# Rotations ahead of the key and value evictions, G cleared in two parts, and the identity copied before the scores

## The reference, cut to what matters

```python
# RWKV-7, per head of 64: the state S is updated token by token
def step(state, inp):
    r_t, w_t, k_t, v_t, kk_t, a_t = inp
    sa = jnp.einsum('bhij,bhj->bhi', state, -kk_t)
    state = (state * w_t[:, :, None, :] + sa[..., None] * (kk_t * a_t)[:, :, None, :]
             + v_t[..., None] * k_t[:, :, None, :])
    return state, jnp.einsum('bhij,bhj->bhi', state, r_t)

# latent attention: 16 heads, 64 plain + 32 rotated features, values of 64
c = hn @ w_down
cq, ckv, kr = jnp.split(c, [384, 640], axis=-1)
q = (rmsnorm(cq, q_norm) @ w_uq).reshape(b, s, 16, 96)
kv = (rmsnorm(ckv, kv_norm) @ w_ukv).reshape(b, s, 16, 128)
q = jnp.concatenate([q_nope, apply_rope(q_rope, positions)], axis=-1)
k_rope = jnp.broadcast_to(apply_rope(kr[:, :, None, :], positions), (b, s, 16, 32))
k = jnp.concatenate([k_nope, k_rope], axis=-1)
o = causal_softmax_attention(q, k, v, 1.0 / math.sqrt(96))
return o.reshape(b, s, 1024) @ w_o
```

## Time and profile before

| | us |
|---|---|
| median of 3 runs (lowest, highest) | 1560.34 (1556.35, 1560.39) |
| the profiled execution | 1560.42 |
| its span | 1558.7 |
| TensorE busy (share of the span) | 1466.2 (94%) |
| VectorE busy | 897.0 (58%) |
| ScalarE busy | 611.8 (39%) |
| GpSimd busy | 161.8 (10%) |
| mean granted clock of TensorE, share of full speed | 0.958 |

### The profile page before, as it was taken

One profiled execution on the slowest core, in us unless ns is written; L12 is line 12 of the kernel. 1 busy time (PEld: TensorE's weight loads), 2 busy tenths in 40 slices (PEclk: granted clock), 3 DMA queues, 4 the chain that ended last, 5 costly groups with the idle time before them and its releaser, 6 DMA issues.

```text
span 1558.7 us, 25630 instructions
## 1 busy us (share of the span) xinstructions
PE 1466.2 (94%) x10804; PEld 1394.0 (89%) x10804; DVE 897.0 (58%) x1167; ACT 611.8 (39%) x722; POOL 161.8 (10%) x149
## 2 busy tenths in 40 slices
PE   4999999899999999999989998999988889999997
PEld 4999999898899999988878878999988778999997
DVE  4655566583356556632563315866676573766665
ACT  3434444434135443411245113444445364344344
POOL 1000000141000000511110000000041051000023
PEclk8999999999999999999989759999998989999998
DMA  8655655332455555524300013555552602555540
GB/s 267 202 188 179 206 169 189 122 126 82 144 176 167 188 188 188 163 85 148 111 1 1 1 61 130 179 180 182 187 162 91 201 4 93 166 181 184 187 135 28
DMA packets 166200, 219.80 MB, mean 141 GB/s; under 512 B 5451, under 2 KB 147020, under 8 KB 165996
## 3 DMA queue, kind: packets, MB, share of 16 engines
q1 hardware_dynamic: 163472, 216.40, 42.3%
q10 hardware_dynamic: 2652, 2.30, 0.5%
HBM read 217.49 MB, written 1.06 MB: 140 GB/s over the span
## 4 chain that ended last, share of the span: by engine, by line
PE 82%; DVE 9%; ACT 4%; issue 3%; POOL 1%; DMA 0%; ACTq 0%; POOLq 0%; SPq 0%; DVEq 0%
PE ps L863 35%; PE ps L903 15%; PE ps L1000 6%; PE ps L839 5%; PE ps L982 2%; PE ps L849 2%; PE ps L1287 2%; PE ps L823 1%; DVE x_second_part L2091 1%; PE ps L1282 1%; PE ps L971 1%; ACT weights_first_parts L1560 1%; PE ps L1425 1%; PE ps L1293 1%; PE ps L855 1%
## 5 line engine op out<-in xcount | busy, mean ns | idle before, releaser
L2192 DVE TENSOR_TENSOR weights_second_parts<-weight_bays,weights_first_parts 128x2048 fp32r<-128x2048 f32 x132 | 301.2, 2289 | 173.2 <-ACT weights_first_parts L1560 172.8
L1560 ACT ACTIVATE weights_first_parts<-weight_bays 128x2048 fp32r<-128x2048 f32 x132 | 252.1, 1918 | 301.9 <-PE ps L863 191.0
L863 PE MATMUL ps<-x_first_part,weights_first_parts 128*128 128x256 f32 x1488 | 210.1, 284 | 1.7 <-DVE weights_second_parts L2192 1.7
L863 PE MATMUL ps<-x_second_part,weights_first_parts 128*128 128x256 f32 x1488 | 208.8, 283 | 0.0
L863 PE MATMUL ps<-x_first_part,weights_second_parts 128*128 128x256 f32 x1488 | 206.5, 282 | 0.0
L863 PEld LDWEIGHTS ps<-x_first_part,weights_first_parts 128*128 128x128 f32 x1488 | 191.8, 192 | 2.7 <-ACT weights_first_parts L1560 1.9
L863 PEld LDWEIGHTS ps<-x_second_part,weights_first_parts 128*128 128x128 f32 x1488 | 191.9, 191 | 0.0
L863 PEld LDWEIGHTS ps<-x_first_part,weights_second_parts 128*128 128x128 f32 x1488 | 189.6, 190 | 0.0
L903 PE MATMUL ps<-hidden_first_part,weights_first_parts 128*128 128x256 f32 x704 | 141.9, 283 | 5.8 <-ACT weights_first_parts L1560 3.7
L903 PE MATMUL ps<-hidden_second_part,weights_first_parts 128*128 128x256 f32 x704 | 141.8, 283 | 0.0
L903 PE MATMUL ps<-hidden_first_part,weights_second_parts 128*128 128x256 f32 x704 | 139.7, 279 | 0.0
(11 more groups left out here) (413 smaller groups left out, 2220.6 us busy)
## 6 DMA issues: line engine op xcount, KB each, us to landing
weight_bays<-in_w_ffn_in SPq DMA_DIRECT2D x44, 1024.0 KB, 5.1
weight_bays<-in_ffn_w_in SPq DMA_DIRECT2D x44, 1024.0 KB, 5.0
weight_bays<-in_w_ffn_out SPq DMA_DIRECT2D x22, 1024.0 KB, 5.1
weight_bays<-in_ffn_w_out SPq DMA_DIRECT2D x22, 1024.0 KB, 5.0
weight_bays<-in_w_in SPq DMA_DIRECT2D x19, 1024.0 KB, 5.3
weight_bays<-in_hyb_w_in SPq DMA_DIRECT2D x13, 1024.0 KB, 5.3
weight_bays<-in_ple_w_gate SPq DMA_DIRECT2D x8, 1024.0 KB, 5.1
weight_bays<-in_w_out SPq DMA_DIRECT2D x4, 1024.0 KB, 5.8
```

Source lines behind the costliest of these rows:

```text
L863: mm = nc.tensor.matmul(dst, w[:, k, j * P:j * P + width], x[:, k], start=(n + k == 0), stop=(n == 2 and k == KD - 1))
L1560: nc.scalar.activation(hi, raw, ACT.Copy).then_inc(*w_hi_ready.inc(f, g, kind, of - g))
L2192: v.tensor_tensor(lo, raw, hi, ALU.subtract).then_inc(*w_lo_d.inc(f, g, kind, of - g))
```

## The change

It does three things.

1. G is cleared in two parts. Elements 2048 to 8191 are cleared once VectorE has written AR (a new event "ar", at which VectorE waits for itself as it did before by a step), elements 0 to 2047, where lw and cc lie, once Bk and Kk are written ("bk"). Before, all of it waited for "bonus".
2. The copy of the identity into Y stands right behind the bonus product, ahead of the wait for G and of the 16 predicated copies. Before, it stood behind them.
3. VectorE's rotations stand in `keep_up` between the query evictions and those of keys and values. Before, they stood behind all evictions.

```diff
--- before.py
+++ after.py
@@ -578,7 +578,7 @@
         def wait_up(eng, bank_no, event):
 
             eng.wait_ge(*(up_a if bank_no % 2 == 0 else up_d).at(*event))
-        def keep_up(eng, parity, split):
+        def keep_up(eng, parity, split, between=None):
 
             done = (up_a, up_d)[parity]
 
@@ -596,6 +596,8 @@
                     copy(dst, bank(b), t).then_inc(*done.inc("q", b // 2, b % 2))
                     if n < 2:
                         split(6 + n)
+            if between:
+                between()
             for (n, t, half), b in UKV.items():
                 if b % 2 == parity:
                     eng.wait_ge(*used_up_to(("ukv", n)))
@@ -1994,8 +1996,11 @@
                     t = slice(tile, tile + tiles)
                     nc.gpsimd.tensor_tensor(xm[0:rows, t], pfT[0:rows, t, 0:SEQ], pfT[0:rows, t, 1:], ALU.subtract).then_inc(*mix_g.inc(key))
 
-                pool.wait_ge(*pre_d.at("bonus"))
-                nc.gpsimd.memset(G[:].rearrange("p a b c d -> p (a b c d)"), 0.0).then_inc(*mix_g.inc("G"))
+                zeroed = G[:].rearrange("p a b c d -> p (a b c d)")
+                pool.wait_ge(*pre_d.at("ar"))
+                nc.gpsimd.memset(zeroed[:, 2048:], 0.0)
+                pool.wait_ge(*pre_d.at("bk"))
+                nc.gpsimd.memset(zeroed[:, 0:2048], 0.0).then_inc(*mix_g.inc("G"))
 
                 def before(t, *event):
 
@@ -2481,7 +2486,8 @@
                 ar = AR.rearrange("p a c n s -> p (a c) n s")
                 two = lambda t: t.rearrange("p a (c s) -> p (a c) s", c=2)
                 v.tensor_tensor(ar[:, :, 0], two(kk), two(dm0), ALU.mult)
-                step(v.tensor_tensor(ar[:, :, 1], two(xm[:, 0:4]), two(dm), ALU.mult))
+                v.tensor_tensor(ar[:, :, 1], two(xm[:, 0:4]), two(dm), ALU.mult).then_inc(*pre_d.inc("ar"))
+                dve.wait_ge(*pre_d.at("ar"))
                 for j in range(RWT):
                     ins = v.scalar_tensor_tensor(xm[:, j], xm[:, j], col("r_k", j), xm[:, 4 + j], ALU.mult, ALU.mult)
                 ins.then_inc(*pre_d.inc("bonus_terms"))
@@ -2490,6 +2496,7 @@
                 dve.wait_ge(*pre_p.at("bonus"))
                 dve.wait_ge(*pre_d.at("bk"))
                 v.tensor_tensor(bonus[:], ps[:, 4:6].rearrange("p b (a s) -> p (b a) s", a=2), xm[:, 8:12], ALU.mult).then_inc(*pre_d.inc("bonus"))
+                step(v.tensor_copy(Y[:].rearrange("p a b c -> p (a b) c"), ident.unsqueeze(1).to_broadcast([P, 16, P])))
                 dve.wait_ge(*mix_g.at("G"))
                 two_masks = masks[:, BEFORE:UPTO + 1].rearrange("p a b -> p (a b)").unsqueeze(1).to_broadcast([P, 2, 2 * P])
                 for n in range(16):
@@ -2506,7 +2513,6 @@
                     mask = masks[:, n].unsqueeze(1).to_broadcast([P, 4, P])
                     if n == 0:
                         dve.wait_ge(*inv_d.at("scores", 15))
-                        step(v.tensor_copy(Y[:].rearrange("p a b c -> p (a b) c"), ident.unsqueeze(1).to_broadcast([P, 16, P])))
                     for g in range(4):
                         if n == 0:
                             data = G[:, g // 2, g % 2 * 4:g % 2 * 4 + 4, 0]
@@ -2625,15 +2631,18 @@
                 v.tensor_scalar(msq[:, 2:4], ps[:, 7, 2:4], 1.0 / 256, EPS, ALU.mult, ALU.add).then_inc(*mean_ready.inc("latent"))
                 dve.wait_ge(*lat_p.at("kr"))
                 v.tensor_copy(krot, ps[:, 6, 0:64].rearrange("p (a b) -> p a b", a=TT)).then_inc(*lat_d.inc("kr"))
-                keep_up(dve, 1, rest_of_mla)
-                dve.wait_ge(*lat_d.at("kr"))
-                dve.wait_ge(*rot_a.at("rot"))
-                step(rotate(krot, [P, TT, 16], cosv[:], sinv[:]))
-                v.tensor_copy(ktok2[:, :, :, 64:96], krot.unsqueeze(2).to_broadcast([P, TT, MH, 32])).then_inc(*lat_d.inc("rotary_key"))
-                dve.wait_ge(*up_a.at("q", 2, 0))
-                dve.wait_ge(*up_d.at("q", 2, 1))
-                cs, sn = (t.unsqueeze(2).to_broadcast([P, TT, MH, 16]) for t in (cosv[:], sinv[:]))
-                rotate(qtok[:, :, :, 64:96], [P, TT, MH, 16], cs, sn).then_inc(*mla_d.inc("rotated"))
+
+                def rotated():
+                    dve.wait_ge(*lat_d.at("kr"))
+                    dve.wait_ge(*rot_a.at("rot"))
+                    step(rotate(krot, [P, TT, 16], cosv[:], sinv[:]))
+                    v.tensor_copy(ktok2[:, :, :, 64:96], krot.unsqueeze(2).to_broadcast([P, TT, MH, 32])).then_inc(*lat_d.inc("rotary_key"))
+                    dve.wait_ge(*up_a.at("q", 2, 0))
+                    dve.wait_ge(*up_d.at("q", 2, 1))
+                    cs, sn = (t.unsqueeze(2).to_broadcast([P, TT, MH, 16]) for t in (cosv[:], sinv[:]))
+                    rotate(qtok[:, :, :, 64:96], [P, TT, MH, 16], cs, sn).then_inc(*mla_d.inc("rotated"))
+
+                keep_up(dve, 1, rest_of_mla, rotated)
                 mask = mats[:, 2].unsqueeze(1).to_broadcast([P, 2, P])
                 for i in range(MH + 2):
                     if i < MH and i % 2:
```

## The result

| | before | after |
|---|---|---|
| median, us (lowest, highest; runs) | 1559.2 (1556.35, 1560.39; 4) | 1544.86 (1542.53, 1546.54; 4) |
| the profiled execution, us | 1560.42 | 1546.54 |
| its span, us | 1558.7 | 1544.8 |
| mean granted clock | 0.958 | 0.966 |

The ratio is 0.991 (95% interval 0.9889 to 0.993): the changed kernel is 0.9% faster, some 14 us. The forecast was 1545.4 us with a range of 1541 to 1551.

A forecast was written before the change was run, and what follows sets the result against it. TensorE held 82% of the chain, so only its waits on VectorE or GpSimd could be won. Terms 9.3 (hybrid mixer) + 5.2 (rotations) + 0.5 (clock) = 15.0 us off 1560.42 gave 1545.4 us, range 1541 to 1551.

The forecast's parts named there:

- clearing and identity copy: first predicated copy sooner: Hybrid mixer, scores: clearing leaves the path, identity copy goes ahead; first predicated copy moves from 782.23 to 776.47, gaining 5.8 us.
- 16 copies at TensorE's full pace: Hybrid mixer, scores: TensorE keeps its full clock, so the predicated copies take 10.0 us instead of 11.3, gaining 1.3 us.
- last copy to the transposes: Hybrid mixer, behind the scores: without the identity copy there, transposes start 1.0 us behind the last copy, not 2.1; gain 1.1 us.
- transposes to M1, by the clock: Hybrid mixer: the clock probably stays up at the 16 transposes, which take about 2.3 us instead of 3.46; 1.1 us taken.
- rotations: first head sooner: Latent attention: rotations run between evictions, so TensorE waits only for the last evictions and starts the first head 5.2 us sooner.
- clock in the first heads: Latent attention, behind the rotations: a full clock after the shorter pause saves between 0 and 2.5 us; 0.5 us taken.
- Port blocked: Rival at the scores: the clearing blocks VectorE's bonus terms at the SBUF port; 2.9 us lost, 1548.3 us; 15%.
- Clock falls in both places as before: Rival at scores and rotations: only the waits go, 8.2 + 5.2 = 13.4 us, giving 1547.0 us; 20%.
- Clock stays down longer: Rival in the inverse's levels: TensorE at the lower clock, matmuls grow by 30 to 50 us, net 1560 to 1580; 3%.
- gain swallowed: Rival at the scores or first head: another, unpriced wait takes most of the gain; about 1553 to 1557 us; 7%.
- both near rivals together: SBUF port blocked at the scores and clock falling at scores and rotations, both at once: 1549.5 us, inside the range.
- The slower rival: Rival in the inverse's levels: the clock stays low there and the kernel ends at 1560 to 1580 us; 3%.

The follow-up runs named there:

- rot_longer: The changed kernel with eight unused 128x512 VectorE products added behind the rotations; median 1543.94 us, ratio 0.9923.
- ident_in_clear: The changed kernel with the identity copy moved right behind the product into Kk, while GpSimd's clearing is under way; median 1542.01 us, ratio 0.9874.
- ident_only: The kernel before with only the identity copy put ahead of the wait for G, still cleared in one piece; median 1556.45 us, ratio 0.9989.
- fill_short: The kernel before with unused matmuls in TensorE's waits, 12 ahead of the fifth pair's scores and 10 ahead of the first head; median 1557.16 us, ratio 0.9987.
- hyb_parts: The kernel before with the clearing in two parts and the identity copy ahead of the scores, rotations as before; median 1547.55 us, ratio 0.994.
- rot_only: The kernel before with only the rotations moved ahead of the key and value evictions; median 1551.53 us, ratio 0.996.

## Why the prediction was right

| term | forecast | measured | by which rows |
|---|---|---|---|
| clearing and identity copy: first predicated copy sooner | 5.8 | 5.85 | 8.24 to 2.39 |
| 16 copies at TensorE's full pace | 1.3 | 1.43 | 11.28 to 9.85 |
| last copy to the transposes | 1.1 | 1.16 | 2.08 to 0.92 |
| transposes to M1, by the clock | 1.1 | 1.02 | 4.25 to 3.23 |
| **sum to the first M1** | **9.3** | **9.46** | 25.85 to 16.39 |
| rotations: first head sooner | 5.2 | 5.24 | 18.24 to 13.00 |
| clock in the first heads | 0.5 | 1.36 | 44.26 to 42.90 |
| **sum of both places** | **15.0** | **16.06** | |

**Point by point.** The clearings took 5.22 and 1.80 us (5.2 and 1.8 forecast) and were over before the bonus product. The slack of the first group of evictions was 2.92 us by VectorE's wait, 2.98 by rot_longer (2.7 forecast). The wait ahead of the first head is 1.80 us. Each term of waiting was right to 0.1 us, because each came from two rows of the same trace whose distance only the order of the work sets.

**The term that was mis-sized** is the clock in the first heads: "Between 0 and 2.5 I take 0.5 us". It measured 1.36. My reasons for the low end were that each head also passes through the other engines, and that the clock might fall in the shorter pause too. Against the first, at the lower level the pace of the first heads was TensorE's (busy 5.00 of 5.00 us), and only at the higher one did TensorE have time to spare (busy 3.24 of 5.00). Against the second, the clock was kept through the pause of 1.8 us.

**The rivals.** *Port blocked* (15%): the bonus terms and both products took their usual times beside a clearing, and ident_in_clear shows on one timeline that the product passes and a copy doesn't. *Clock falls in both places as before* (20%): it did not, in either. At the transposes the table gives the reason more firmly than I had it. In the five kernels that copy the identity behind the scores, TensorE pauses twice (some 1.3 and 1.1 us) and the step to M1 takes 4.1 to 5.2 us; in the eight that copy it ahead, it pauses once and the step takes 3.22 to 3.24. I had argued from the length of the pause alone; the runs show that taking the second of two away decides here: ident_only keeps the long pause ahead of the scores and doesn't lose the clock at the transposes, fill_short has no long pause and loses it. *Clock stays down longer* (3%) and *gain swallowed* (7%): neither appeared in any profile; the levels behind ran at 1.00 in the changed kernel, where under 0.8 would have told against me. Two of the prediction's figures for rivals are wrongly added up: both near rivals together give 1545.4 + 2.9 + 1.6 = 1549.9 us, not 1549.5, and a loss of 30 to 50 us against a gain of 15 gives 1575 to 1595 us, not 1560 to 1580. Neither touches the forecast or its range.

**Why the total is lower than the sum.** 16.06 us in the two places is not the 13.88 between the profiled executions. The rest of the program gave back 2.2: +5.15 ahead of the hybrid mixer, -2.17 between the first M1 and the end of its stretch, +1.60 and -2.39 in the two stretches behind. I had no term for any of these, and the forecast of the total came as close as it did (1.1 us) in part because an under-sized term and these differences offset each other. Of the 2.17, 1.50 us is one event, which a timeline of TensorE shows in the kernel before and, below, in the changed one:

```profile
843.32 5.33 PE L1287 MATMUL ps<-arena 128*128 128x128 f32 x32 [2.33 <-ACT arena L1808]
```

```profile
839.01 3.84 PE L1289 MATMUL ps<-arena 128*128 128x128 f32 x32 [2.33 <-ACT arena L1810]
```

The same 32 matmuls, behind the same pause of 2.33 us, take 5.33 us in the one and 3.84 in the other. It is not the hybrid parts: hyb_parts, which has both, shows the slow form, and rot_only, which has neither, the fast one.

**Open.** From the first M1 matmul to the solve it takes 70.2 to 70.7 us in all six traced kernels without the moved rotations and 68.7 in all seven with them; the 32 matmuls of this event take 5.33 to 5.47 us in the six and 3.84 in the seven. So clean a split is hardly chance, though the rotations come 400 us later and I know of nothing by which they could act on it; nor did I test it. If it belongs to the change, 1.5 us of the gain has a cause that this document doesn't show. Only the changed kernel was profiled twice, with the same pattern both times; both profiled executions were the slowest of their four (1546.54 and 1546.77 us, with others down to 1539.95), so how often the clock falls at each place in other executions isn't known. The slower rival was not provoked: no experiment tried to bring the inverse's levels down to 1.2 GHz.

## What to carry to other kernels

Look for work that stands behind a wait only by its place in the code: its operands were ready, and its engine idle, somewhere earlier. Price such a move by two rows of one trace (when the operands are ready, when the next work is late), and name what is late next; this gave every term of waiting to 0.1 us, while the total of a kernel varied by several. Of several short pauses of TensorE close together, taking one away can be worth more than its length.
